# Row pitch of the split-weight ring: 2048 to 2112 bytes in a two-block transformer kernel

## The reference

```
block 1: hn = rms_norm(x); proj = hn @ w_in           (q, k, v of two attentions, two gates)
         x += (sigmoid(gate_a) * (attA @ w_branch_a) + sigmoid(gate_b) * (attB @ w_branch_b)) @ w_out
         x += (silu(conv(hn2 @ w_up)[gate]) * conv(hn2 @ w_up)[up]) @ w_ffn_down
block 2: h = rms_norm(x); z = h @ w_in_2              (a gated recurrence, a forgetting attention, two gates)
         logf = log_sigmoid(z_f + f_bias); c = cumsum(logf)      (8 heads, 512 tokens)
         s = q k^T * scale + c[t] - c[s]; ...
         x += merged @ w_out_2; x += (silu(hf @ w_gate) * (hf @ w_up)) @ w_down
         x += sigmoid(hp @ w_ple_gate) * (p @ w_ple_proj)
```

## Time and profile before

| | us |
|---|---|
| median of 3 runs (lowest, highest) | 1734.41 (1732.42, 1734.86) |
| the profiled execution's own time | 1730.57 |
| its span, first to last instruction | 1728.8 |
| PE busy (matmuls) | 1695.1 (98%) |
| POOL busy | 767.7 (44%) |
| ACT busy | 666.8 (39%) |
| DVE busy | 594.4 (34%) |

### The profile page before, as it was taken

The page is one execution under the profiler, slowest core; times in us unless marked ns, Lnnn a source line. Parts: engine busy times, 40 slices in busy tenths (PEclk is TensorE's granted clock), DMA queues, the critical chain, the costliest instruction groups (busy, mean ns, idle before and its releaser), DMA issues.

```text
span 1728.8 us, 22714 instructions
## 1 busy us (share of the span) xinstructions
PE 1695.1 (98%) x7752; PEld 1344.1 (78%) x7752; DVE 594.4 (34%) x963; ACT 666.8 (39%) x1151; POOL 767.7 (44%) x605
## 2 busy tenths in 40 slices
PE   7999999999999999999999999999999999999998
PEld 5776777677788888888678877777777888888877
DVE  4055513324343333300466432554423111110144
ACT  5233364233354444422443434523334333332342
POOL 7444432224364444444567423222346444444442
PEclk9999999999999999999999999999999999999999
DMA  4421121112243333323222223221223333333312
GB/s 150 122 87 49 50 74 56 49 55 83 65 116 98 97 97 97 98 97 94 78 74 74 68 61 110 67 56 49 80 79 103 96 95 96 101 106 98 93 56 95
DMA packets 103208, 145.58 MB, mean 84 GB/s; under 512 B 11094, under 2 KB 56895, under 8 KB 102991
## 3 DMA queue, kind: packets, MB, share of 16 engines
q1 hardware_dynamic: 102958, 142.30, 27.7%
q10 hardware_dynamic: 160, 2.11, 0.3%
HBM read 142.24 MB, written 2.13 MB: 84 GB/s over the span
## 4 chain that ended last, share of the span: by engine, by line
PE 89%; DVE 4%; ACT 3%; issue 2%; POOL 2%; DMA 1%; SPq 0%; DVEq 0%; ACTq 0%
PE bank L1484 76%; PE bank L1427 4%; PE bank L1404 3%; PE bank L1412 1%; DVE work L1320 1%; PE bank L1609 1%; POOL w_lo L617 1%; PE bank L1582 1%; ACT L799 1%; POOL h_lo L467 1%; DMA w_raw<-in_w_in 1%; ACT h_hi L859 0%; DVE h_lo L467 0%; PE bank L1630 0%; DMA xtok<-in_x 0%
## 5 line engine op out<-in xcount | busy, mean ns | idle before, releaser
L617 POOL TENSOR_TENSOR w_lo<-w_raw,w_hi 128x512 fp32r<-128x512 f32 x516 | 682.2, 1330 | 809.5 <-ACT w_hi L792 806.8
L792 ACT ACTIVATE w_hi<-w_raw 128x512 fp32r<-128x512 f32 x516 | 318.8, 629 | 675.6 <-PE bank L1484 599.3
L1484 PE MATMUL bank<-h_hi,w_lo 128*128 128x512 f32 x1376 | 550.4, 400 | 7.3 <-ACT hk L882 2.8
L1484 PE MATMUL bank<-h_hi,w_hi 128*128 128x512 f32 x1376 | 537.4, 391 | 0.0
L1484 PE MATMUL bank<-h_lo,w_hi 128*128 128x512 f32 x1376 | 537.1, 390 | 0.0
L1484 PEld LDWEIGHTS bank<-h_hi,w_lo 128*128 128x128 f32 x1376 | 259.0, 188 | 90.7 <-issue 22.9
L1484 PEld LDWEIGHTS bank<-h_hi,w_hi 128*128 128x128 f32 x1376 | 258.8, 188 | 55.2
L1484 PEld LDWEIGHTS bank<-h_lo,w_hi 128*128 128x128 f32 x1376 | 259.3, 188 | 54.1 <-issue 2.9
L1484 PE MATMUL bank<-g_hi,w_lo 128*128 128x512 f32 x352 | 137.0, 389 | 0.0
L1484 PE MATMUL bank<-g_hi,w_hi 128*128 128x512 f32 x352 | 136.9, 389 | 0.0
L1484 PE MATMUL bank<-g_lo,w_hi 128*128 128x512 f32 x352 | 136.9, 389 | 0.0
(11 more groups left out here) (262 smaller groups left out, 1765.8 us busy)
## 6 DMA issues: line engine op xcount, KB each, us to landing
w_raw<-in_w_in SPq DMA_DIRECT2D x168, 256.0 KB
w_raw<-in_w_ffn_up SPq DMA_DIRECT2D x88, 256.0 KB
w_raw<-in_w_ffn_down SPq DMA_DIRECT2D x88, 256.0 KB
w_raw<-in_w_ffn_gate SPq DMA_DIRECT2D x88, 128.0 KB
w_raw<-in_w_ffn_up SPq DMA_DIRECT2D x88, 128.0 KB
w_raw<-in_w_out SPq DMA_DIRECT2D x32, 256.0 KB
w_raw<-in_w_branch_b SPq DMA_DIRECT2D x16, 256.0 KB
w_raw<-in_w_branch_a SPq DMA_DIRECT2D x16, 256.0 KB
```

The source lines that it names most:

```text
L617: e.tensor_tensor(w_lo[:, pos % SPLIT_SLOTS, :], w_raw[:, pos % RAW_SLOTS, :], w_hi[:, pos % SPLIT_SLOTS, :].bitcast(F32), ALU.subtract).t ...
L792: e.activation(w_hi[:, pos % SPLIT_SLOTS, :], w_raw[:, r, :], ACT.Copy).then_inc(hi_full, 1)
L1484: mm = e.matmul(ps[banks + n][:, :], l, r, start=k == 0 and i == 0, stop=k == p.kc - 1 and i == 2)
```

## The change

Rows of `w_hi` and `w_lo` become 528 elements (2112 bytes) apart, of which the first 512 are used. Row s of `w_hi` then begins 64 s bytes past a multiple of 2 KB, row s of `w_lo` 512 + 64 s bytes past one (because `w_hi` is 512 bytes longer). `w_raw` stays. All readers and writers name the first 512 columns. `cT` is no longer a tensor of its own but the row `fx[:, 0, :]`. The small tensors that follow the rings move up by 1,024 bytes and end at base + 108,736, so U stays at base + 110,592 and nothing in it moves.

```diff
-        w_hi = place("w_hi", [P, SPLIT_SLOTS, S], F32R)
-        w_lo = place("w_lo", [P, SPLIT_SLOTS, S], F32R)
+        w_hi = place("w_hi", [P, SPLIT_SLOTS, S + 16], F32R)
+        w_lo = place("w_lo", [P, SPLIT_SLOTS, S + 16], F32R)
...
-        cT = place("cT", [NH, S])
+        cT = fx[:, 0, :]
...
-                e.tensor_tensor(w_lo[:, pos % SPLIT_SLOTS, :], w_raw[:, pos % RAW_SLOTS, :],
-                                w_hi[:, pos % SPLIT_SLOTS, :].bitcast(F32), ALU.subtract).then_inc(lo_full, 1)
+                e.tensor_tensor(w_lo[:, pos % SPLIT_SLOTS, 0:S], w_raw[:, pos % RAW_SLOTS, :],
+                                w_hi[:, pos % SPLIT_SLOTS, 0:S].bitcast(F32), ALU.subtract).then_inc(lo_full, 1)
...
-                e.activation(w_hi[:, pos % SPLIT_SLOTS, :], w_raw[:, r, :], ACT.Copy).then_inc(hi_full, 1)
+                e.activation(w_hi[:, pos % SPLIT_SLOTS, 0:S], w_raw[:, r, :], ACT.Copy).then_inc(hi_full, 1)
...
-                    e.dma_start(c_dram, cT[:, :]).then_inc(ff["saved"], 16)
+                    e.dma_start(c_dram, cT).then_inc(ff["saved"], 16)
...
-                    e.tensor_scalar(cT[:, :], fx[:, 2, :], -1.0, None, ALU.mult).then_inc(ff["c"], 1)
+                    e.tensor_scalar(cT, fx[:, 2, :], -1.0, None, ALU.mult).then_inc(ff["c"], 1)
...
-                    ops = [(x_hi[:, c], w_lo[:, pos, :]), (x_lo[:, c], w_hi[:, pos, :]), (x_hi[:, c], w_hi[:, pos, :])]
+                    ops = [(x_hi[:, c], w_lo[:, pos, 0:S]), (x_lo[:, c], w_hi[:, pos, 0:S]), (x_hi[:, c], w_hi[:, pos, 0:S])]
```

## The result

The change made the kernel slower: 1752.27 us median of three runs (1752.13 to 1754.60) against 1734.41 us, a ratio of 1.0115 with a 95% interval of 1.0100 to 1.0129. The profiled execution took 1752.27 us with a span of 1750.5 us, 21.7 us more than the span of before. The medians differ by 17.9 us; the spans differ by more because the profiled execution of before was itself 3.8 us under its median. The time is outside the forecast range, and on the side of the prediction's first rival.

The account below looks back on a forecast made before the run. TensorE was taken as the bound, with 6192 ring matmuls x 226.6 ns = 1403 us of the span. All terms were 0, summing to no change from the median: 1734.4 us, range 1730 to 1739.5 us.

Parts of the forecast that it names:

- Rival 1: TensorE's ring matmuls get slower off the grid: 6192 x 3.8 ns = +23.5 us, 1758 us; chance 0.04.
- TensorE's reads of the ring: Matmuls and loads from the ring: same count and shape, only start addresses move; cost taken as 0.
- bounds of -11.6 and +3.8 ns: Per ring matmul: below, a plain float32 pass of 215 ns against 226.6; above, L1590's excess if the address caused it.
- The three equal windows: 100 us windows in up1, down1 and up2 into down2, each 443 ring matmuls, read as showing no address effect.
- the change of instruction pattern: At L1590's 24 matmuls, 230.4 ns each: claimed source of the 3.8 ns excess, instead of the address.
- clause on the 52 moving rows: In rival 1: if only the 52 slots with a moving ring row pay, 624 matmuls x 3.8 = +2.4 us, unseen.
- the parts of ScalarE, GpSimd, `cT` and the small tensors: ScalarE's copy, GpSimd's subtraction, cT's multiply into fx and the small tensors' 1 KB move: each forecast at 0.
- the windows named as the test: Ring matmuls in 100 us of the changed kernel: 443 if forecast right, 436 for rival 1, 467 for rival 3.
- Rival 3: TensorE's ring matmuls get faster, equal places in 2 KB having cost 11.6 ns: -71.8 us, 1662.6 us; chance 0.02.

Follow-up runs that it names:

- The run with 2304: Changed kernel with a ring pitch of 2304 bytes and U at the next multiple of 256 bytes; 1731.54 us against 1732.82, ratio 0.9996.
- The aligned L1590: Kernel before, with only wf_hi and wf_lo given 256-byte rows so L1590's eight-column loads start on multiples of 256 bytes; one execution, 1733.34 us.

## Why the prediction was wrong

The step that failed is the first, *TensorE's reads of the ring*, where I took 0 out of bounds of -11.6 and +3.8 ns; it measured +4.2 ns in the windows, above even the upper bound, and 21.7 us on the span.

- "If two accesses in the same place of a 2 KB period hurt each other, the four tiles and the phases would differ." The sentence looked for a difference among rows that could not show one: every start in the earlier trace rows is a multiple of 256 bytes from every other. The three equal windows were one sample of distance, not many. The run with 2304 shows that they would have stayed equal.
- "I put that down not to the address but to the change of instruction pattern." had the only displaced loads among the rows, with an excess of 3.8 ns, close to the mean of 4.2 that the changed kernel then paid. I explained it away by the earlier trace rows. The aligned L1590 has none of it left. The excess of the earlier trace rows, after a pause and at distance 0, exists as well, but is another thing, as the start of phase hi in that run shows; what causes it no run here tests.
- The Trainium skill, "SBUF — State Buffer", section "A bandwidth-pool intuition that's wrong (but worth ruling out)", makes contention a matter of locked ports, and from that the prediction got 0; the measured 4.2 ns decide against that use of it here. The Trainium skill, "TensorE: Matmul & The Clock Gate", section "Step-by-step: what each phase is for", says that loading the next tile's weights takes no read bandwidth from the running matmul. These runs do not fit an independence of the two reads: the matmul's interval hangs on where the load reads relative to it, with 128 columns and with 8. Whether it is read bandwidth that is lost, no run shows.
- Rival 1 named the place of the loss, the sign and nearly the size (1758 for 1752 us), with a chance of 0.04 that was far too small: it had the one row that spoke about addresses on its side. It did not name the mechanism: it charged for a start off the grid, and with all tensors 64 bytes off the grid nothing is lost. That its price fits is partly luck, since L1590's loads go through eight distances and the ring's rows through four. Its clause on the 52 moving rows alone was wrong, as both directions pay.
- Right: the parts of ScalarE, GpSimd, `cT` and the small tensors at 0, and the windows named as the test, in which 435 could be read. Rival 3's gain did not show in any run: no placement brought a row under 226.6 ns.

Is the changed kernel explained by the distances? Uniform runs have 226.7 (0), 233.3 (+64), 232.4 (+128) and, at -64, which is +192, 228.9 ns. Their mean, 230.3, covers 3.6 of the 4.0 ns of the changed kernel (226.7 to 230.7 by the starts), whose rows sample just these. More than half of the 0.4 left is a change between rows: row 0 follows a row at another distance, and its first four intervals have 228.5, 232.4, 231.0 and 227.1 ns before they settle at 226.7, which is 12 ns in 48 matmuls. What makes two reads at certain distances hinder each other stays open. So does whether a load meets the matmul before its own or its own: the runs with only `w_lo` or only `h_lo` displaced spread the loss over all three intervals, and single intervals form patterns of their own.

## What to carry to other kernels

Keep stationary and moving operands at equal addresses modulo 256 bytes when matmuls run back to back; pitches and starts that were 16 to 128 bytes off cost 0.7 to 1.8% of this kernel, a pitch of 2304 nothing. This was seen with float32r operands, 512 moving columns and one load a matmul; other types and shapes were not run. Uniform rows in a profile say nothing of a case that none of them samples: list first what values the disputed variable takes in the trace, and give the one odd row the weight of the only witness. When a kernel is bound by one instruction at one rate, a few ns on it outweigh every other term.

## What the hardware showed

- Two operands in SBUF, both read by TensorE, interact with a period of 256 bytes in their distance: 226.7 ns a matmul at 0; 233.3 at +32 and +64; 232.4 at +128; 228.9 at -64 (rings against activations, the four long phases).
- Moving both together by 64 bytes changes nothing (443 in the window), and a small load pays too: 8 columns, over eight distances 32 bytes apart, cost 3.8 ns a matmul on average, where 128 columns over the same eight distances (pitch 2080, 433 in the window) cost 5.2.
- Alternating distances cost more than a constant one: 13.3 ns for one stationary operand in three at +64, against 6.7 ns each when all are; 16 ns for one moving operand in three displaced (distance -64), against 2.2.
